# Four transformer layers on one core: mixture-of-experts weights used as plain float32, two experts side by side in TensorE, instead of one expert at a time in three float32r passes

## The reference, cut to what matters

```python
grp = scores.reshape(-1, N_EXPERT_GROUPS, EXPERTS_PER_GROUP)
g_sel = jnp.argmax(jnp.sum(lax.top_k(grp, TOP_K)[0], axis=-1), axis=-1)
...                       # the two best experts inside the best group of four
for e in range(N_EXPERTS):
    h = jax.nn.silu(xt @ w_gate[e]) * (xt @ w_up[e])
    y = y + gate[:, e:e + 1] * (h @ w_down[e])
```

## Time and profile before

| what | value |
|---|---|
| median of 3 runs | 2125.27 us (2123.26 to 2125.39) |
| profiled execution, first to last instruction (span) | 2120.6 us |
| time around the span, by the median | 4.7 us |
| the four expert stages, from the first expert's matmul to the end of the last scatter | 284.8, 284.8, 300.8, 285.2 us: 1155.6 us |
| bytes moved | 574.65 MB, of them 500.19 MB weights over SP's queue |
| mean granted TensorE clock | 0.963 of full |

### The profile page before, as it was taken

One profiled execution on the slowest core, in us unless ns is written; L12 is line 12 of the kernel. 1 busy time (PEld: TensorE's weight loads), 2 busy tenths in 40 slices (PEclk: granted clock), 3 DMA queues, 4 the chain that ended last, 5 costly groups with the idle time before them and its releaser, 6 DMA issues.

```text
span 2120.6 us, 24733 instructions
## 1 busy us (share of the span) xinstructions
PE 1994.9 (94%) x9388; PEld 1588.8 (75%) x9388; DVE 1610.3 (76%) x2023; ACT 1126.7 (53%) x1144; POOL 87.4 (4%) x136
## 2 busy tenths in 40 slices
PE   8999899999899997999998988899999788999997
PEld 5677688888647776888887875788888664788885
DVE  1787689889646868988886275889889654888987
ACT  1323366777322234767763363477777341676774
POOL 1111000000110110000000000000000000000000
PEclk9999899999999998999998999799999998899998
DMA  9777669999884854989994501588889521799994
GB/s 383 288 290 295 209 244 349 342 360 357 316 332 159 313 203 159 375 321 357 360 366 146 208 31 40 189 327 336 339 322 350 199 80 50 265 349 341 359 358 172
DMA packets 56414, 574.65 MB, mean 271 GB/s; under 512 B 5856, under 2 KB 9952, under 8 KB 24032
## 3 DMA queue, kind: packets, MB, share of 16 engines
q1 hardware_dynamic: 34704, 500.19, 62.3%
q0 software_dynamic: 15264, 59.78, 7.7%
q10 hardware_dynamic: 6320, 12.97, 1.8%
HBM read 569.77 MB, written 3.15 MB: 270 GB/s over the span
## 4 chain that ended last, share of the span: by engine, by line
PE 84%; DVE 11%; issue 3%; ACT 2%; DMA 0%; POOL 0%; POOLq 0%; ACTq 0%; DVEq 0%
PE bank L788 81%; DVE ring_parts L1950 3%; PE bank L820 2%; DVE work L1950 1%; DVE mix L2092 1%; DVE mix L1950 1%; ACT work L1464 1%; DVE small L1950 1%; ACT mix L1464 0%; DVE work_parts L1950 0%; ACT work_parts L1464 0%; PE bank L916 0%; DMA xT<-in_xT_in 0%; DVE oT L2128 0%; DVE small L2101 0%
## 5 line engine op out<-in xcount | busy, mean ns | idle before, releaser
L1950 DVE TENSOR_TENSOR ring_parts<-ring,hi_ring_parts 128x2048 fp32r<-128x2048 f32 x422 | 947.6, 2285 | 103.6 <-ACT hi_ring_parts L1464 102.9
L1464 ACT ACTIVATE hi_ring_parts<-ring 128x2048 fp32r<-128x2048 f32 x422 | 798.3, 1914 | 265.9 <-PE bank L788 190.3
L788 PE MATMUL bank<-hi_ring_parts,tokens 128*128 128x512 f32 x2048 | 662.9, 393 | 3.0 <-DVE mix L1950 1.7
L788 PEld LDWEIGHTS bank<-hi_ring_parts,tokens 128*128 128x128 f32 x2048 | 384.6, 188 | 85.0 <-DVE mix L1950 3.4
L788 PE MATMUL bank<-ring_parts,tokens 128*128 128x512 f32 x1024 | 399.1, 390 | 0.0
L788 PE MATMUL bank<-hi_ring_parts,work_parts 128*128 128x512 f32 x1024 | 326.4, 390 | 0.0
L1464 ACT ACTIVATE work<-bank 128x512 f32<-128x512 f32 (+6 forms) x207 | 108.6, 527 | 285.0 <-PE bank L788 273.4
L788 PEld LDWEIGHTS bank<-hi_ring_parts,work_parts 128*128 128x128 f32 x1024 | 192.3, 188 | 40.1
L788 PEld LDWEIGHTS bank<-ring_parts,tokens 128*128 128x128 f32 x1024 | 192.6, 188 | 37.6
L788 PE MATMUL bank<-ring_parts,work_parts 128*128 128x512 f32 x512 | 199.3, 389 | 0.0
L788 PE MATMUL bank<-ring,xT 128*128 128x512 f32 (+2 forms) x352 | 139.2, 555 | 1.8 <-DVE xT L2481 1.8
(11 more groups left out here) (232 smaller groups left out, 2257.4 us busy)
## 6 DMA issues: line engine op xcount, KB each, us to landing
ring<-in_weights SPq DMA_DIRECT2D x237, 2048.0 KB, 8.7
hi_ring<-in_ada POOLq DMA_DIRECT2D x38, 512.0 KB, 12.0
mod_rows<-in_ada POOLq DMA_DIRECT2D x25, 512.0 KB, 5.9
work<-in_ada POOLq DMA_DIRECT2D x22, 512.0 KB, 6.0
work<-in_vecs POOLq DMA_DIRECT2D x8, 1024.0 KB, 5.5
mix<-in_ada POOLq DMA_DIRECT2D x11, 512.0 KB, 5.5
work<-bias_rows ACTq DMA_DIRECT2D x4, 1024.0 KB, 8.0
ring<-in_weights SPq DMA_DIRECT2D x2, 1024.0 KB, 8.0
```

The source lines that it names most:

```text
L788: ins = nc.tensor.matmul(o, lhsT, rhs, start=start, stop=stop)
L1464: return nc.scalar.activation(o, i, f, **kw)
L1950: return v.tensor_tensor(o, a, b, op)
```

## The change

Experts are handled in rounds (`rounds_of`). A round of two experts has 64 places for each: the first expert's tokens are columns 0 to 63 of the stationary side and its output is on partitions 0 to 63 of the bank, the second's are 64 to 127. For each chunk of the contraction PE issues a matmul for the one expert and then one for the other, with 64 stationary columns and 512 moving ones, in plain float32 on the weights as they lie in the ring. The splits by ACT and DVE are gone, for the tokens as for the weights. A piece now holds, for both experts of the round, the same half of a matrix, and comes in two loads of 1024 KB each. Layers 0 and 1 have 8 such rounds. Layers e and o have 9: experts 0 and 1, then two rounds with one expert each, in 128 places, and six rounds of two. There DVE ranks experts 2 to 15 by their counts of tokens (`positions`), the two fullest take the single rounds, and SP reads from the table `order` which expert's weights to load. Tokens are gathered with all four terms of one job in one bank, for round 0 alone and then for two rounds at a time; every round is scattered by itself. The ring keeps its four slots (SLOTS = 4). What does not fit into its places is computed in a branch that runs all 16 experts on all 256 tokens.

```diff
+def rounds_of(tag):
+    pair = [(p, p + 1) for p in range(0, NEXP, 2)]
+    return [pair[0], (2,), (3,), *pair[2:]] if tag in SORTED else pair
...
+    order = [("g", 0), ("u", 0), ("d", 0), ("g", 1), ("u", 1)]
+    for r in range(1, n - 1):
+        order += [("g", r + 1)] + ([("d", r), ("u", r + 1)] if r < n - 2 else [("u", r + 1), ("d", r)])
+    return order + [("d", n - 1)]
...
+def ring_plan():
+    slot, full, need = [], [], []
+    held, landed = [-1] * SLOTS, [0] * SLOTS
+    for tag in TAGS:
+        first, linear = MOE_FIRST[tag], LINEAR[tag]
+        last_split = max(PARTS[f"{tag}.{name[:-1]}"][0] for name in linear if name.endswith("/"))
+        for m in range(first - len(linear), first + NMOE):
+            if m == first:
+                held[RING:] = [last_split] * (SLOTS - RING)
+            usable = range(SLOTS) if m >= first else range(RING)
+            j = min(usable, key=lambda k: held[k])
+            pair = m >= first and len(ROUNDS[tag][MOE_PIECES[tag][m - first][1]]) == 2
+            landed[j] += 32 if pair else 16
+            slot.append(j)
+            full.append(landed[j])
+            need.append(2 * (held[j] + 1))
+            held[j] = m
+    return slot, full, need
...
+                def sides(what, r, h, chunks):
+                    if len(kinds[r]) == 1:
+                        w = take(what, r, h).rearrange("p (c n) -> p c n", c=chunks)
+                        return [(range(chunks), slice(0, P), w)]
+                    w = take(what, r, h).rearrange("p (a c n) -> p a c n", a=2, c=chunks // 2)
+                    return [(range(chunks // 2 * h, chunks // 2 * (h + 1)), slice(CAP * a, CAP * (a + 1)), w[:, a])
+                            for a in range(2)]
...
+                def gate_up(what, r, parts=None):
+                    name = f"{tag}.{what}{r}"
+                    for h in range(len(kinds[r])) if parts is None else parts:
+                        o = begin(name) if h == 0 else psum[banks.jobs[name][0]]
+                        of = sides(what, r, h, DC)
+                        for k, c in enumerate(of[0][0]):
+                            for _, cols, w in of:
+                                ins = mm(o[cols, :], tokens_of(tag, r)[:, c, cols], w[:, k, :], c == 0, c == DC - 1)
+                        release[0] += 2
+                        if c == DC - 1:
+                            end(name, ins)
...
+                    for h in range(len(kinds[r])) if parts is None else parts:
+                        o = [begin(name) if h == 0 else psum[banks.jobs[name][0]] for name in names]
+                        of = sides("d", r, h, HC)
+                        chunks = list(enumerate(of[0][0]))
+                        final = chunks[-1][1] == HC - 1
+                        for n, (k, c) in ([(n, kc) for n in range(2) for kc in chunks] if final and r == last else
+                                          [(n, kc) for kc in chunks for n in range(2)]):
+                            for _, cols, w in of:
+                                ins = mm(o[n][cols, :], ehT[:, r % 2, c, cols], w[:, k, n * 512:(n + 1) * 512],
+                                         c == 0, c == HC - 1)
+                            if c == HC - 1:
+                                end(names[n], ins)
+                        release[0] += 2
...
-                def three(o, a_hi, a_lo, b_hi, b_lo, start, stop):
-                    mm(o, a_hi, b_hi, start, False)
-                    mm(o, a_hi, b_lo, False, False)
-                    return mm(o, a_lo, b_hi, False, stop)
...
-                        for c in range(DC // 2):
-                            t = (slice(None), DC // 2 * h + c, slice(None))
-                            ins = three(o, tok_hi[b][t], tok_lo[b][t], hi[:, c, :], lo[:, c, :],
-                                        h == 0 and c == 0, h == 1 and c == DC // 2 - 1)
...
+                gate(0)
+                gate_up("u", 0)
+                gather(1)
+                places(1)
+                turn_hidden(0)
+                down(0)
+                gate(1)
+                gate_up("u", 1)
+                scatter(0)
+                for r in range(1, last):
+                    two = len(kinds[r + 1]) == 2
+                    gate(r + 1, (0,)) if two else None
+                    turn_hidden(r)
+                    gate(r + 1, (1,) if two else None)
+                    if r < last - 1:
+                        down(r)
+                        if gathered_ahead(tag, r):
+                            gather(gathered_ahead(tag, r))
+                            places(gathered_ahead(tag, r))
+                        gate_up("u", r + 1)
+                        scatter(r)
                     else:
-                        down(k)
-                    if not last and not up_first(k + 1):
-                        up(k + 1)
-                    if k % per == per - 1:
-                        scatter(k // per)
+                        gate_up("u", r + 1)
+                        down(r, (0,))
+                        turn_hidden(r + 1)
+                        down(r, (1,))
+                down(last, (0,))
+                scatter(last - 1)
+                down(last, (1,))
+                scatter(last)
...
+                step(tt(greater, key.unsqueeze(1).broadcast_to([P, NEXP, NEXP]),
+                        key.unsqueeze(2).broadcast_to([P, NEXP, NEXP]), ALU.is_ge))
+                step(v.tensor_reduce(pos, greater, AX.X, ALU.add))
+                step(tt(at, pos.unsqueeze(1).broadcast_to([P, NEXP, NEXP]),
+                        cs("iota")[:, 0:NEXP].unsqueeze(2).broadcast_to([P, NEXP, NEXP]), ALU.is_equal))
+                step(tt(greater, at, cs("third").unsqueeze(1).broadcast_to([P, NEXP, NEXP]), ALU.mult))
+                step(v.tensor_reduce(key, greater, AX.X, ALU.add))
...
-            def split_expert(tag, j, halves=(0, 1)):
-                for half in halves:
-                    part = Half(tag, j, half)
-                    dve.wait_ge(hi_ready, part.n)
-                    tt(part.lo, part.raw, part.hi, ALU.subtract).then_inc(lo_ready, 1)
...
+            def load_expert(tag, m, found):
+                first = MOE_FIRST[tag]
+                what, r, h = MOE_PIECES[tag][m - first]
+                for p in ROUNDS[tag][r]:
+                    if tag in SORTED and p >= 2 and p not in found:
+                        k = SORTED.index(tag)
+                        sp.wait_ge(order_ready, k + 1)
+                        found[p] = sp.value_load(order[0:1, k * NEXP + p:k * NEXP + p + 1], min_val=0, max_val=3 * (NEXP - 1))
+                if NEED[m]:
+                    sp.wait_ge(halves_done, NEED[m])
+                into, full = ring_slot(SLOT[m]), slot_full[SLOT[m]]
+                for a, p in enumerate(ROUNDS[tag][r]):
+                    one = len(ROUNDS[tag][r]) == 1
+                    dest = into if one else into[:, a * HALF:(a + 1) * HALF]
+                    cols = slice(0, PIECE) if one else slice(h * HALF, (h + 1) * HALF)
+                    if p in found:
+                        src = weights[bass.ds(found[p] + (first + WHAT[what]), 1), :, cols].rearrange("m p n -> p (m n)")
+                    else:
+                        src = weights[first + 3 * p + WHAT[what], :, cols]
+                    sp.dma_start(dest, src).then_inc(full, 16)
```

More of the change, by code:

```diff
@@ L51 @@
 RING = 4
+SLOTS = 4
 PIECE = 4096
@@ L201, in constants @@
     put("half", np.full((P, 16), -0.5))
+    e = np.arange(NEXP)
+    put("tie", np.tile(np.where(e < 2, 1.0e6 - e, NEXP - 1 - e), (P, 1)))
+    put("third", np.tile(3 * e, (P, 1)))
     return c
@@ L957, in experts @@
             def experts(tag):
-                layer, per = MOE_LAYER[tag[0]], PER_SET[tag[0]]
-                rows = in_set(tag)
-                n = rows.shape[2]
+                layer, kinds, sets = MOE_LAYER[tag[0]], ROUNDS[tag[0]], SETS[tag[0]]
+                last = len(kinds) - 1
                 every = cs("ones")[:, 0:1].broadcast_to([P, P])
@@ L1567, in attention @@
                         output_high(units[k - 4])
-            def split_expert(tag, j, halves=(0, 1)):
-                for h in halves:
-                    part = Half(tag, j, h)
-                    act.wait_ge(slot_full[part.slot], part.full)
-                    if part.free:
-                        act.wait_ge(halves_done, part.free)
-                    fn(part.hi, part.raw, ACT.Identity).then_inc(hi_ready, 1)
             def src_high(tag, T, ready_row):
@@ L1688, in experts @@
-                y_hi(sets - 1)
+                gathered(0)
+                places(0)
+                sig(0)
+                gathered(1)
+                places(1)
+                hidden(0)
+                y_hi(0)
+                sig(1)
+                for r in range(1, last):
+                    hidden(r)
+                    sig(r + 1)
+                    if r == last - 1:
+                        hidden(r + 1)
+                    y_hi(r)
```

(3 more changed lines are left out.)

957 lines of the change are left out of this document (329 added, 628 removed).

## The result

The changed kernel takes 1954.19 us (median of four runs, 1949.94 to 1956.12), the kernel before 2124.57 (2123.26 to 2125.39). The ratio is 0.9199, with an interval of 0.9186 to 0.9213. I had predicted 1975 us, range 1930 to 2120. The sign and the mechanism were right; two terms of the sum were off, with opposite signs: the price of a weight piece was too high and the fixed part of a stage too small.

A forecast was written before the change was run, and what follows sets the result against it. PE was taken to bound the kernel, with loads close behind. Savings of 39.9 us twice, 44.3 and 28.7, less 2, gave -150.8: the span 2120.6 becomes 1969.8, plus 4.7 makes 1975 us; range 1930 to 2120.

The forecast's parts named there:

- The fixed part of a stage: Expert stages, layers 0 and 1: 3.4 us to the first free slot, 1.9 for a load, 3.4 and 3.0 at the end.
- Half-width matmuls, 0.43 us: Expert stages on PE: matmuls with 64 stationary columns run at once in both column halves, 0.43 us each, not 0.86.
- The loads become the bound: Expert stages: PE needs only 204.5 us in layers 0 and 1, 227.6 in e and o, so the loads end last.
- A piece costs 5.3 us: Weight loads in the expert stages: 2.097 MB takes 5.3 us, the middle of 5.05 and 5.56.
- Between the stages: Routing ahead of the expert stages: 0 in layer 0, +2 us in layer 1, 0 in e and o.
- Turns (1): Expert stages: column halves take turns, half-width matmuls cost 0.86 us, PE ends last again, 2455 us; chance 0.12.
- Partial overlap (2): Expert stages: column halves overlap in part, 0.54 us a half-width matmul, 2000 us and up to 2120; chance 0.12.
- Slow loads (3): Expert stages: loads stay as slow or get slower, 5.9 us a piece (353 GB/s), 2064 us; chance 0.06.
- The clock (4): Expert stages: PE rests between pieces and its clock falls; mean 0.75 cancels the saving, below is slower; chance 0.05 slower.
- Two loads of 1024 KB in place of one, priced at 0: Weight loads of two-expert rounds: splitting a piece into two loads costs 0, with the piece price's ends to hold it.
- The first gather, 0 taken and at most 5 us: Token gather: 128 moving columns in place of 256 save 0, at most 0.43 - 0.26 us a matmul, 5 us a layer.
- Changes between half and full width: PE in the expert rounds: some six a round at 0.16 us, 1 us a round, hidden beside the loads.

The follow-up runs named there:

- e1: Changed kernel with all matmuls of a piece's first expert issued before all of the second's, instead of one of each in turn; 2025.7 us (ratio 0.9539).
- e2: Changed kernel with idle copies on ScalarE and subtractions on VectorE added in the middle rounds of the expert stages; 2007.37 us (ratio 0.9448).
- e6: Kernel before without the splitting of the experts' weights on ScalarE and VectorE, all three passes kept; 2111.53 us (ratio 0.9944).
- e5: Kernel before without the splitting of the experts' weights and with two float32r passes in place of three; 1906.4 us (ratio 0.8977).

## Why the prediction was right, and which term was off

**Half-width matmuls, 0.43 us.** Right: 0.456 (3.65 / 8), 6% above the bound of full overlap. e1 shows that it is overlap, and that it depends on order, which I had given as the reason. That only neighbours in the queue overlap was too narrow (above). The estimate of 0.54 us, by the Trainium skill's figure for three column tiles (TensorE: Matmul & The Clock Gate, Measured speedup vs the span model), was too high for two: 0.86 / 0.456 is 1.89x. The Trainium skill's "Up to 2×" for a dimension of at most 64 (TensorEngine Tiling (Array Packing), Theoretical Speedup; it does not stand in Key Properties, where I placed it) fits.

**The loads become the bound.** Right: PE waits for the ring 63 times, and the DMA share is 0.98 in layers 0 and 1. Two readings on the way there were weak. That SP waited for PE for 1892 us was no proof that PE ended last, and the sign "SP no longer for PE" did not come, though the loads now set the pace.

**A piece costs 5.3 us.** This is the step that failed. It took the middle between 5.05 (the projections) and 5.56 us (377 GB/s per share in the stages), reasoning that PE's fast reading or the splits slowed the transfers. Measured: 4.98 us. e2 and e6 show that the splits slow nothing, e5 that float32r doesn't. The 377 was not a price of the transfer but a mark of a stage that TensorE bounds, where packets at the start of each load take longer. Over the 150 pieces of the sum, 0.32 us each, that is 48 us too much.

**The fixed part of a stage.** Too small, which hid half of the error. In layer 0 the stage runs from 275.5 to 511.5:

```profile
275.50:280.00 4.50, 4.50 (x17) 1.46 (x19) 2.34 (x10) 1.61 (x3) 0.00 (x0) 0.72 0.00 0
```

```profile
281.26 7.67 SPq L2660 DMA_DIRECT2D ring<-in_weights  x6
```

```profile
499.60 3.65 PE L747 MATMUL bank<-ring,work 128*64 128x512 f32 x16 [1.33 <-DMA ring<-in_weights]
503.19 2.11 PE L747 MATMUL bank<-work_parts 128*128 128x512 f32 x8
505.23 3.65 PE L747 MATMUL bank<-ring,work 128*64 128x512 f32 x16
```

The first load is issued at 281.26, 5.7 us after the start and not 3.4. The first piece is multiplied at a granted clock of 0.72, so partly at 1.2 GHz: its first three pairs start 0.78 to 0.91 us apart and the others 0.43, which is 1.3 us, and some 1.1 us pass between its last matmul and the issue. Then 44 x 4.98 = 219.1 us of loads, 4.9 until the last piece's matmuls at 505.23 where I had 1.9, and 6.3 to the end as predicted (3.4 + 3.0). Together 236.0: fixed part 16.9 where I had 11.7, 5.2 too small. In layer 1 it is 6.3 too small by the same reading, in e (254.4 - 31 x 4.98 = 100.0 against 92.2) 7.8, in o 8.6; there the single rounds hold the loads back for longer than the 83.9 us of PE work that I counted: in layer e the 17th piece lands 91.3 us after the stage's start. Sum of the four: 28 us.

The low clock at the start was not in my sum at all, because before the change no stage had it. There the granted clock rose to 1.00 some 3 us ahead of every stage. In the changed kernel it rises 2.5, 4.2, 4.6 and 5.2 us into the stage, and the first load is issued 5.7, 6.6, 6.8 and 7.1 us after the start where I had 3.4, 12.6 of the 28 us. These are the starts of layer 1's stage, before and after:

```profile
832.40:842.00 9.60, 9.60 (x44) 7.96 (x44) 6.87 (x10) 8.89 (x8) 0.00 (x0) 1.00 0.27 80
```

```profile
785.70:795.00 9.30, 9.30 (x35) 2.94 (x37) 2.33 (x10) 1.64 (x4) 0.00 (x0) 0.77 0.18 45
```

Half of the 16.5 us at the lower level, about 8 us of the 28, is what the clock costs here, by an estimate from these rows. Why it rises later, no run isolates.

**Between the stages.** +2 predicted, all of it ahead of layer 1; +0.4 measured in all by the windows of the earlier trace rows, which begin 0.1 to 0.2 us after each stage's first matmul, and +1.0 by the matmuls themselves: 271.5 us before and 274.2 after ahead of layer 1, and 0.3 to 1.0 us less ahead of each of the others. But e6, with the routing of before, has 273.5 there too, so that the +2.7 is the routing is not shown. The last stage's end to the kernel's end is 13.8 us in both.

The sum: -150.8 predicted; -48 for the pieces, +28 for the fixed parts, -1.6 between, gives -172.4, and the spans differ by 172.6. The two errors had opposite signs, and that they half cancelled is luck: with the piece priced right and the fixed parts as I had them I would have said 1927 us, below my own range.

**Rivals.** Turns (1) would have been 2455; e1, the nearest thing to it, is 2025.7. Partial overlap (2): no, 0.456 us and not 0.54. Slow loads (3): no, 421 GB/s. The clock (4): not inside the stages, only at their starts (above). PE rests between pieces and is busy for 7.4 of 10 us in places, and the granted clock stays at 1.00, the 2.4 GHz level (the changed kernel's window from 480):

```profile
480.00:490.00 10.00, 7.37 (x34) 2.53 (x32) 0.75 (x1) 0.20 (x1) 0.00 (x0) 1.00 1.01 421
```

**Two loads of 1024 KB in place of one, priced at 0.** The changed kernel moves 421 GB/s, e5 with whole 2048 KB loads 427: 0.07 us a piece, some 13 us over the 180 pieces that come in two loads, if it is the size that does it. The two kernels differ in TensorE's work too, but the packets' records point at the size: in the changed kernel's stretch from 1300 to 1340, which has both kinds, a packet of 8 KB takes 309 ns in the median and one of 16 KB 611, so 424 and 429 GB/s. No run changes the size alone.

**The first gather, 0 taken and at most 5 us.** 6.9 us in place of 5.5 in layer 0: all of it lies at the lower clock, where half of it did before.

**Changes between half and full width.** From 499.60 to 503.19 eight pairs take 3.59 us, and eight scatter matmuls 2.04 to 505.23, where 8 x 0.43 and 8 x 0.227 are 3.44 and 1.82: about 0.2 us a change where I had 0.16. It is hidden beside the loads, as predicted.

## What to carry to other kernels

Two independent matmuls with at most 64 stationary columns each, in different column halves and issued near each other, cost little more than one (0.91 us against 0.86): where experts, heads or batches are at most half full, try them side by side in plain float32. Here such a pair costs less than two experts in three float32r passes each (6 x 0.227 = 1.36 us). Float32r passes side by side were not tried, nor whether they overlap as well. GB/s divided by the DMA share is not the rate that the transfers could reach: read that rate from a stretch in which the loads end last, or from the median time of a packet, and take it as the price when a change makes the loads the bound. Once they are, count what they can do before a stage begins and where the consumer is slow: two more slots and another place for the slow rounds brought 57 us here, a third of what the change itself did.

## What the hardware showed that I had not expected

- Overlap of column halves reaches over more than the next matmul: blocks of two cost nothing (1956 us), blocks of four 0.10 us a half-width matmul (0.56 against 0.456), where overlap of neighbours alone would give 0.645 and no overlap 0.86.
- In float32r, 128 moving columns instead of 256 saved next to nothing, at either clock. The first gather's float32r matmuls with 128 moving columns, in the changed kernel at a granted clock of 0.50 (1.2 GHz), start 0.213 us apart (two in each row):

```profile
269.60 0.63 PE L747 MATMUL bank<-work_parts,x_parts 128*128 128x128 f32 x2
270.03 0.63 PE L747 MATMUL bank<-work_parts 128*128 128x128 f32 x2
```

  and those of before with 256 columns 0.21 us at the same place, before the clock rises (four in each row):

```profile
270.23 1.05 PE L788 MATMUL bank<-work_parts,x_parts 128*128 128x256 f32 x4
271.08 1.05 PE L788 MATMUL bank<-work_parts 128*128 128x256 f32 x4
```

  At a granted clock of 1.00 the same matmuls with 128 columns, in the changed kernel's last gather of layer 0, start 0.113 us apart, where 256 columns take 0.120:

```profile
458.64 0.39 PE L747 MATMUL bank<-work_parts,x_parts 128*128 128x128 f32 x2
458.87 0.38 PE L747 MATMUL bank<-work_parts 128*128 128x128 f32 x2
```

- Packets at the start of a load take longer where few loads are queued: in layer 0's stage of the kernel before, which TensorE bounds, 798 of 5197 packets of 16 KB took over 700 ns where the median is 611; with the loads as the bound (e5), 16 of 5219.

- ScalarE and VectorE reading and writing SBUF for some 70% of the time take nothing measurable from the weight loads: 421 GB/s with and without.
